# The last product of each unit behind the next unit's first, in the seven-product matmuls of a two-model forward pass

## The reference

```python
u = jnp.square(jax.nn.relu(h @ mlp_w1[i])) @ mlp_w2[i]           # twice, 1024 -> 4096 -> 1024

def _swiglu(x, w_gate, w_up, w_down):                            # four times, 1024 -> 2816 -> 1024
    return (jax.nn.silu(x @ w_gate) * (x @ w_up)) @ w_down
```

## Time and profile before

| what | value |
|---|---|
| median of 3 runs | 3332.48 us (3332.04 to 3334.54) |
| profiled execution, first to last instruction | 3327.9 us |
| what lies around the span, by the median | 4.6 us |
| PE busy | 3224.8 us (97%) |
| DVE, ACT, POOL busy | 2011.6, 1456.2, 872.9 us (60%, 44%, 26%) |
| PE's waits for DVE's additions at line 2277 | 17.9 us, 18 times |

### The profile page before, as it was taken

How to read it: one execution, slowest core, us unless ns; L and a number is a source line. 1 busy time by engine, 2 the same in 40 slices (tenths; PEclk the granted TensorE clock), 3 DMA queues, 4 the chain that set the end, 5 groups by cost and what they waited for, 6 DMA issues and landing times.

```text
span 3327.9 us, 47776 instructions
## 1 busy us (share of the span) xinstructions
PE 3224.8 (97%) x20089; PEld 2867.4 (86%) x20092; DVE 2011.6 (60%) x3009; ACT 1456.2 (44%) x2244; POOL 872.9 (26%) x401
## 2 busy tenths in 40 slices
PE   8999999999999999999999999999999999999998
PEld 6887889988668899888999788999999998789998
DVE  6568755445866544576747636574766476367646
ACT  4465445443534544454434324453454343235433
POOL 3210033321400233303232430323222323312232
PEclk9999999999999999999999999999999999999999
DMA  4310233331102333323222322332332323223332
GB/s 133 105 50 26 99 98 112 101 119 58 64 26 89 102 114 102 109 71 125 92 85 97 114 81 84 115 102 83 115 102 89 103 83 125 76 89 108 96 96 76
DMA packets 239814, 308.97 MB, mean 93 GB/s; under 512 B 8336, under 2 KB 168096, under 8 KB 239088
## 3 DMA queue, kind: packets, MB, share of 16 engines
q1 hardware_dynamic: 236016, 291.41, 26.8%
q0 software_dynamic: 3584, 14.52, 1.2%
HBM read 303.80 MB, written 2.10 MB: 92 GB/s over the span
## 4 chain that ended last, share of the span: by engine, by line
PE 78%; DVE 16%; ACT 4%; issue 2%; DMA 0%; POOL 0%; DVEq 0%; ACTq 0%; POOLq 0%
PE bank L598 24%; PE bank L600 24%; PE bank L599 24%; DVE wlo L2082 3%; ACT whi L1322 2%; PE bank L979 1%; DVE wraw L2104 1%; DVE xl L2155 1%; PE bank L618 1%; DVE raw_w L2104 1%; PE bank L1261 1%; PE bank L1252 1%; PE bank L1186 0%; DVE st L2113 0%; DVE wkk_o L2899 0%
## 5 line engine op out<-in xcount | busy, mean ns | idle before, releaser
L3140 POOL TENSOR_TENSOR wlo<-wraw,whi 128x1024 fp32r<-128x1024 f32 (+2 forms) x209 | 531.1, 2545 | 1374.3 <-ACT whi L1322 1374.1
L598 PE MATMUL bank<-xh,whi 128*128 128x256 f32 (+1 forms) x2456 | 721.0, 294 | 46.4 <-DVE zt L2277 17.9
L1322 ACT ACTIVATE whi<-wraw 128x1024 fp32r<-128x1024 f32 (+3 forms) x426 | 441.1, 1039 | 678.7 <-PE bank L600 546.2
L600 PE MATMUL bank<-xh,wlo 128*128 128x256 f32 (+1 forms) x2456 | 715.7, 291 | 0.0
L599 PE MATMUL bank<-xl,whi 128*128 128x256 f32 (+1 forms) x2456 | 711.8, 290 | 0.0
L3140 POOL TENSOR_TENSOR wlo<-raw_w,whi 128x1024 fp32r<-128x1024 f32 (+1 forms) x126 | 300.6, 2389 | 867.4 <-ACT whi L1322 867.4
L598 PEld LDWEIGHTS bank<-xh,whi 128*128 128x128 f32 x2456 | 464.5, 189 | 66.8 <-issue 27.1
L598 PE MATMUL bank<-whi,uh_w 128*128 128x512 f32 x1216 | 473.9, 390 | 0.0
L600 PE MATMUL bank<-whi,ul_w 128*128 128x512 f32 x1216 | 473.3, 389 | 0.0
L599 PEld LDWEIGHTS bank<-xl,whi 128*128 128x128 f32 x2456 | 464.5, 189 | 10.2
L599 PE MATMUL bank<-wlo,uh_w 128*128 128x512 f32 x1216 | 473.2, 389 | 0.0
(11 more groups left out here) (392 smaller groups left out, 5009.7 us busy)
## 6 DMA issues: line engine op xcount, KB each, us to landing
wraw<-in_w_in SPq DMA_DIRECT2D x26, 1024.0 KB, 5.1
wraw<-in_ffn_w_down SPq DMA_DIRECT2D x20, 1024.0 KB, 5.0
raw_w<-in_ffn_w_down SPq DMA_DIRECT2D x20, 1024.0 KB, 5.1
raw_w<-in_mlp_w SPq DMA_DIRECT2D x19, 1024.0 KB, 5.1
wraw<-in_mlp_w SPq DMA_DIRECT2D x17, 1024.0 KB, 5.3
wraw<-in_ffn_w_gate SPq DMA_DIRECT2D x32, 512.0 KB, 4.6
raw_w<-in_ffn_w_gate SPq DMA_DIRECT2D x32, 512.0 KB, 4.8
raw_w<-in_ffn_w_up SPq DMA_DIRECT2D x32, 512.0 KB, 4.4
```

The costliest lines, as they stand in the source:

```text
L598: M.matmul(o, lh, rh, start=start, stop=False, skip_group_check=more)
L600: return M.matmul(o, ll, rh, start=False, stop=stop, skip_group_check=more)
L1322: A.activation(hi, raw, ACT.Copy).then_inc(*k.w_hi.inc(("hi", j)))
L3140: G.tensor_tensor(lo[:, 0:n], raw[:, 0:n], hi[:, 0:n].bitcast(F), ALU.subtract).then_inc(*k.w_lo.inc(("lo", j)))
```

## The change

The order of a block's products is changed: product 4 of a unit comes after product 1 of the next unit. The last unit of a block ends with its own product 4 as before. All engines and the plan of the weight parts follow the same function.

```diff
 def product_order(n):
 
-    return [(u, p) for u in range(n) for p in (1, 5, 6, 2, 7, 3, 4)]
+    order = []
+    for u in range(n):
+        order.append((u, 1))
+        if u:
+            order.append((u - 1, 4))
+        order += [(u, p) for p in (5, 6, 2, 7, 3)]
+    return order + [(n - 1, 4)]
```

## The result

The changed kernel took 3347.98 us (median of 4 runs, 3347.45 to 3350.19) against 3332.26 us for the kernel before in the same session (4 runs, 3329.50 to 3334.54): a ratio of 1.0047, interval [1.0033, 1.0062]. It is slower by 15.7 us. The forecast was 3328.8, its range ended at 3336, and "slower" had a chance of 0.07.

What follows compares the result with a forecast made beforehand. PE, busy 97% of the span, was taken as the bound, so only its waits could be won. 9.0 + 2.5 - 7.8 = 3.7 us gained gave 3324.2 + 4.6 = 3328.8 us, range 3320 to 3336.

Steps and rivals of the forecast that it cites:

- What bounds the kernel: Whole kernel: PE busy 97% of the span; only its idle time can be won, including 17.9 us waiting at line 2277.
- First units: First unit of four gated feed-forwards: moved product 4 starts without its wait, gaining 4 x 2.26 = 9.0 us.
- the narrow pair's loss: Narrow pair in a first gated block: DVE also has a wide down-weight part, so 1.3 us lost, four times.
- Blocks of four wide units: Four such blocks: sum for p4 joins DVE's chain, yet low parts stay ahead; gain 4 x 0.63 = 2.5 us.
- Narrow units: Third, narrow units of first and third gated blocks: DVE's chain comes late; 4 x 0.65 + 4 x 1.3 = 7.8 us lost.
- The second rival: Narrow pairs: POOL's part starts before DVE's sum for the last p4, which waits by the lock; 3335.8 us, chance 0.17.
- the MLP block, taken as nothing: MLP blocks (6 moves): nothing waited before and cover stays over 0.5 us; effect nothing, 2 us loss if cover is gone.
- Third rival: Wide units: DVE's amount of work sets sum22, so the 2.26 us return at p5 or p6 next; 3338 us, chance 0.07.

Runs made afterwards that it cites:

- run 1: Only product 4 of the first unit of the four gated feed-forwards moves (4 moves of 42), against the kernel before; 3326.67 us, ratio 0.9986.
- run 4: The full change, with POOL's low part for a block's last product 3 waiting for DVE's sum for the last product 4; 3334.41 us, 1.0008 of the kernel before.
- run 5: The kernel before, no moves; DVE's sum for a block's last product 4 waits for POOL's low part of the last product 3; 3347.33 us, ratio 1.0048.
- run 10: The full change, with DVE's sum for a moved product 4 made again with product 3's part, as before; 3335.47 us, 1.0013 of the kernel before.
- 11: run 10 plus run 4's wait on POOL; 3322.73 us, 0.9975 of the kernel before.
- run 2: Only product 4 of each block's last unit but one moves (18 moves of 42), against the kernel before; 3351.30 us, ratio 1.0059.
- run 3: The full change without the move of the last unit but one's product 4 (24 of 42 moves remain); 3345.14 us, 1.0039 of the kernel before.
- run 12: run 11's order, sums and POOL wait in first and four-wide gated blocks alone, the rest as in the kernel before; 3318.67 us, ratio 0.9962.
- 7: The kernel before, no moves; at product 7 DVE makes sum22 ahead of its part preparation; 3362.57 us, ratio 1.0091.
- 8: Run 7's edit on the full change with POOL waiting for the last product 4's sum and the last unit's sum22; 3340.08 us, ratio 1.0023.

## Why the prediction was wrong

**What bounds the kernel** was right: PE's idle time is the currency, and the waits at line 2277 in wide units go by the moves.

**First units.** The 2.26 us went as forecast, with p4 behind p1 next and no gap. They are no gain of the block: run 1 has 0.2 us left of them, because the second unit's p4 and the third unit's p7 and p4 then wait. In the changed kernel too a first block is only 0.2 us shorter; there the stop of 1.6 us at its last product 4 takes most of it. The forecast followed DVE to p6 next and stopped there. With the narrow pair's loss the term came out right by chance, 3.8 forecast and 3.9 measured: 3.1 of the 3.9 are two spells of low clock that the forecast didn't count.

**The step that failed** is the end of the block, in "Blocks of four wide units" and "Narrow units". "Worked through, the tightest low part still comes 1.5 us ahead of its product" asked each low part how far it is ahead of PE; it never asked the sum for the last p4 how far it is ahead of POOL. That distance was 0.70 us in the kernel before, and DVE became later by more. The second rival had this very mechanism, but only for narrow pairs: with it the whole was to be 3.3 us slower, and a third block 1.3 us longer. Its turn of places is there, by 0.09 us (3297.46 and 3297.55). It costs 2.6 us, because the delay hits twice: the multiply that now starts beside POOL's down part wasn't in the sum. The forecast's own path for the narrow pair, a wait of 0.70 us left at p4 and then late parts for p6 next and p2 next that make it 0.65 us longer, came out too dear: no wait at p4, 0.33 us at each of the other two, and the pair even but for its last product. In four-wide blocks the term is -4.3 instead of +2.5, and the MLP block, taken as nothing, costs 2.9 us. A third of that is its last p4, by the same way (DVE's sum at 496.67 takes 3.41 us). The rest is a wait of p7 for ACT: the readers of the moved p4's quarter now stand ahead of a high part, which starts at 495.47 where it was at 494.18. Run 4 keeps this 1.7 us wait, so POOL isn't its cause; that the readers are wasn't tested alone.

**The places are most of the price.** Run 5 pays 15.3 us for the places without a move; run 4 takes 13.3 of 15.7 us off with the moves left; run 10 takes the turn away in four-wide blocks by DVE's order alone, and 11 in the others by POOL's wait. In four-wide blocks it needs the moves as well: with the places turned alone (run 5) or with the last move alone (run 2) they take 80.3 to 80.7 us, not 81.5.

**Clock.** The forecast had no term for it. In the profiled executions the changed kernel's three spells at the ends of third blocks cost 4.8 us and the two of the kernel before 3.1, so the clock is little of the difference between these two; in runs 3, 4 and 11 it is a third to a half of the effect.

**Third rival**, that DVE's work as a whole is the limit, is wrong as it was put: nothing comes back at p5 or p6 next of the wide units, and run 12 wins. But runs 1, 7 and 8 show it where the forecast took cover as free; in run 1 1.9 of the 2.26 us come back, further down the block.

## What to carry over

When an operation is moved on an engine that shares an access with another, write down for each pair of neighbours who starts first, and by how much, up to the end of the stage: a lead of 0.1 to 0.7 us that is lost costs most of the other operation's time, at every operation behind it that meets the next one. If moved work has some grace, look for the first piece that has the delay without the grace. A wait on the engine that has time, so that the urgent one stays first, can bring more than the reordering itself, and a reordering is best kept to the blocks whose own length it shortens.

## What the runs showed of the hardware

- A DVE operation with two SBUF inputs that started 0.06 to 1.5 us behind a POOL operation, while this was running, ended 0.15 us less than its own length after it: 1.07 us after for an operation of 1.21 (2603.20), 0.54 for one of 0.69 (3297.55), 0.28 for one of 0.42 (3301.08). In a row the engines take turns: DVE's part at 2601.05 waited for POOL's first, POOL's second (2602.53) for that, and DVE's sum for POOL's second.
- With starts 0.01 us apart (run 10) DVE went first; with 0.06 and 0.09 us POOL did.
- After one stop of 2.0 to 2.6 us in a full stream at 2.4 GHz, PE's granted clock was 0.50 for some 3.4 us in some places, at 1.5 to 1.6 us each: in 2 of 4 first blocks of the kernel before, 3 of 4 third blocks after, 8 of 8 first and third blocks in run 3, and none of 4 first blocks in run 2, where the stop was 2.27 us as in the kernel before. While it was low, a matmul started each 0.21 us instead of 0.12. It stayed at 1.00 behind the fourth third block, although that wait at 3304.12 was as long. What decides is open.
